# Broadcasts and sums in rounded parts, z gates in couples, a new order of filler units, and merge levels on half the columns, in a chain of transformer blocks

## The reference

```python
def first_block(...):
    x = x + 0.5 * swiglu(rms_norm(x, ffn1_norm), ...)
    x = x + hybrid_mixer(x, ...)
    x = x + 0.5 * swiglu(rms_norm(x, ffn2_norm), ...)
    return rms_norm(x, final_norm)

def second_block(...):
    for i in range(2):
        h = h + (gdn_mixer, sb_mixer)[i](rms_norm_2(h, ln_mix[i]), ...)
        h = h + swiglu_2(rms_norm_2(h, ln_ffn[i]), ...)
        h = h + (p[i] @ ple_w_proj[i]) * jax.nn.sigmoid(rms_norm_2(h, ln_ple[i]) @ ple_w_gate[i])
```

```python
    decay_mat = jnp.exp(jnp.where(causal, G[..., :, None] - G[..., None, :], -jnp.inf))
    a_low = jnp.where(strict, beta[..., None] * kk * decay_mat, 0.0)
    rhs = jnp.concatenate([v * beta[..., None], k * (beta * jnp.exp(G))[..., None]], axis=-1)
    sol = lax.linalg.triangular_solve(a_low + eye, rhs, lower=True, unit_diagonal=True)
```

## Time and profile before

| | us |
|---|---|
| median of 3 runs | 2642.24 (2640.12 to 2644.57) |
| profiled execution, its own time | 2639.76 |
| its span, first to last instruction | 2638.0 |
| PE busy | 2593.3 |
| DVE, ACT, POOL busy | 1041.8, 1089.7, 1060.8 |
| mean granted clock | 0.995 |

### The profile page before, as it was taken

How to read it: one execution, slowest core, us unless ns; L and a number is a source line. 1 busy time by engine, 2 the same in 40 slices (tenths; PEclk the granted TensorE clock), 3 DMA queues, 4 the chain that set the end, 5 groups by cost and what they waited for, 6 DMA issues and landing times.

```text
span 2638.0 us, 32543 instructions
## 1 busy us (share of the span) xinstructions
PE 2593.3 (98%) x12090; PEld 2100.3 (80%) x12090; DVE 1041.8 (39%) x1477; ACT 1089.7 (41%) x1567; POOL 1060.8 (40%) x466
## 2 busy tenths in 40 slices
PE   9999999999999999999999999999999999999999
PEld 7888887776888888777878878888877777888887
DVE  4212223966522122787456542122372344211224
ACT  5222233678432223565445542223355464222233
POOL 4444443222444444335334344444443222444444
PEclk9999999999999999999999999999999999999999
DMA  4232332111232222222000122322322112222233
GB/s 158 95 101 93 102 125 77 62 56 57 88 103 98 94 96 95 80 80 80 17 25 25 33 96 95 104 89 95 103 89 79 56 48 80 96 96 96 95 103 113
DMA packets 61719, 222.68 MB, mean 84 GB/s; under 512 B 6704, under 2 KB 6832, under 8 KB 61488
## 3 DMA queue, kind: packets, MB, share of 16 engines
q1 hardware_dynamic: 60928, 218.07, 25.0%
q10 hardware_dynamic: 688, 3.15, 0.3%
HBM read 219.10 MB, written 2.10 MB: 84 GB/s over the span
## 4 chain that ended last, share of the span: by engine, by line
PE 91%; DVE 6%; issue 2%; ACT 1%; DMA 0%; SPq 0%; DVEq 0%; ACTq 0%
PE ps L358 13%; PE ps L360 13%; PE ps L359 13%; PE ps L385 6%; PE ps L384 6%; PE ps L383 6%; PE ps L646 2%; PE ps L647 2%; PE ps L648 2%; PE ps L1471 1%; PE ps L1502 1%; PE ps L2187 1%; PE ps L1412 1%; PE ps L1414 1%; PE ps L1413 1%
## 5 line engine op out<-in xcount | busy, mean ns | idle before, releaser
L2470 POOL TENSOR_TENSOR w_lo<-raw,w_hi 128x1024 fp32r<-128x1024 f32 x405 | 981.9, 2426 | 1471.5 <-ACT w_hi L403 1471.5
L403 ACT ACTIVATE w_hi<-raw 128x1024 fp32r<-128x1024 f32 x405 | 424.9, 1050 | 468.2 <-PE ps L385 294.2
L358 PE MATMUL ps<-x_hi,w_hi 128*128 128x512 f32 x1536 | 600.7, 391 | 5.1 <-DVE x_lo L436 5.1
L359 PE MATMUL ps<-x_lo,w_hi 128*128 128x512 f32 x1536 | 597.7, 389 | 0.0
L360 PE MATMUL ps<-x_hi,w_lo 128*128 128x512 f32 x1536 | 597.6, 389 | 0.0
L358 PEld LDWEIGHTS ps<-x_hi,w_hi 128*128 128x128 f32 x1536 | 288.3, 188 | 69.9 <-DVE x_lo L436 6.7
L359 PEld LDWEIGHTS ps<-x_lo,w_hi 128*128 128x128 f32 x1536 | 288.3, 188 | 60.8 <-issue 1.4
L360 PEld LDWEIGHTS ps<-x_hi,w_lo 128*128 128x128 f32 x1536 | 288.3, 188 | 60.0
L383 PE MATMUL ps<-mid_hi,w_hi 128*128 128x512 f32 x736 | 286.3, 389 | 0.0
L384 PE MATMUL ps<-mid_lo,w_hi 128*128 128x512 f32 x736 | 286.3, 389 | 0.0
L385 PE MATMUL ps<-mid_hi,w_lo 128*128 128x512 f32 x736 | 286.3, 389 | 0.0
(11 more groups left out here) (371 smaller groups left out, 3814.1 us busy)
## 6 DMA issues: line engine op xcount, KB each, us to landing
raw<-in_units_dram SPq DMA_DIRECT2D x406, 512.0 KB, 3.5
h<-in_x_t_dram SPq DMA_DIRECT2D x4, 512.0 KB, 6.5
toep<-in_rel_table_dram ACTq DMA_DIRECT2D x1, 2048.0 KB, 9.1
out_dram<-h SPq DMA_DIRECT2D x4, 512.0 KB, 5.6
p_f<-in_p_t_dram ACTq DMA_DIRECT2D x2, 512.0 KB, 3.6
const<-in_constants_dram SPq DMA_DIRECT2D x1, 832.0 KB, 7.5
vec<-in_vectors_dram SPq DMA_DIRECT2D x1, 137.5 KB, 2.2
```

The lines of the kernel that those rows point to most:

```text
L358: nc.tensor.matmul(out, hi, x_hi[:, k, :], start=(k == 0), stop=False)
L359: nc.tensor.matmul(out, hi, x_lo[:, k, :], start=False, stop=False)
L403: nc.scalar.activation(w_hi[:, n % W_SLOTS, :], raw[:, n % RAW_SLOTS, :], ACT.Copy).then_inc(s_whi, 1)
L2470: nc.gpsimd.tensor_tensor(w_lo[:, n % W_SLOTS, :], raw[:, n % RAW_SLOTS, :], w_hi[:, n % W_SLOTS, :].bitcast(F32), ALU.subtract).then_inc( ...
```

## The change

1. *Broadcasts of mixers 1 and 2.* The rows are split into hi and lo parts which lie in one tile (`cs_parts`: hi in partitions 0 to 15, lo from 64; `g_parts`: hi from 0, lo from 64), and one fp32r product with K = 80 (K = 104) spreads their sum; its weights `sel` have two ones in a column. For that DVE does three instructions at x == 6 of mixer 1, ACT one and DVE two in mixer 2.
2. *z gates.* All of PE's gate pieces stand one m earlier; `z_silu` runs for two m at once between two decays; at m = 6 and 7 the pieces of an output unit take the place of gate pieces.
3. *Filler order.* In pair 1, gate 4 comes ahead of the output unit.
4. *Convolution tile 23* and its silu stand behind level 0 of pair 0.
5. *Merge levels.* Only half the columns of each block pattern hold anything new. Each 128x128x128 product becomes two with 64 weight columns and 64 moving columns (every second group of b columns), the two written to the two halves of the partitions. ACT's copy to `em`, DVE's subtraction and POOL's mask work on 256 columns instead of 512, and ACT writes zeros over the columns of `em` that the last level left (two copies a level). The turning to `tm` stays at 512 columns.
6. *Square sums of mixer 3.* hi and lo parts and two fp32r products; DVE squares, ACT copies to hi, DVE subtracts for lo.

The core of the diff:

```diff
...
-FILLS = ((("gate", 0), ("gate", 1), ("gate", 2)), (("gate", 3), ("out", 0, 0), ("gate", 4)),
+FILLS = ((("gate", 0), ("gate", 1), ("gate", 2)), (("gate", 3), ("gate", 4), ("out", 0, 0)),
...
+        sel = place("sel", 144 * KB + 1280 + len(MASKS) * P * 4, [P, 40], F32R)
...
+                    pe.wait_ge(s_sel, 1)
+                    pe.wait_ge(s_csp, 3)
                     pe.wait_ge(s_pt, 24)
                 elif x == 1:
                     pe.wait_ge(s_conv, 11)
                 else:
                     pe.wait_ge(s_m, x - 1)
-                nc.tensor.matmul(ps[:, SPREAD[x % 2], :], ident[0:SSD_HEADS, x:x + 1].to_broadcast([SSD_HEADS, P]), cs_row[:, :],
+                nc.tensor.matmul(ps[:, SPREAD[x % 2], :], sel[0:64 + SSD_HEADS, x:x + 1].to_broadcast([64 + SSD_HEADS, P]), cs_parts[:, :],
...
-            take(gates, 8)
+            take(gates, 16)
...
                 if m < 7:
                     x_turn(m + 1)
                     broadcast(2 * m + 2)
+                if m < 6:
                     take(gates, 4)
+                else:
+                    out_unit(n_t, 0, 0, (0, 1) if m == 6 else (2, 3))
+                if m < 7:
                     broadcast(2 * m + 3)
-                else:
-                    out_unit(n_t, 0, 0, (0, 1))
                 y_pair(m)
-                if m < 7:
+                if m < 6:
                     take(gates, 4)
             assert next(gates, None) is None
-            out_unit(n_t, 0, 0, (2, 3))
...
             z_silu(0)
+            z_silu(1)
             for m in range(8):
                 if m < 7:
                     decays(2 * m + 2)
+                if m in (2, 4, 6):
+                    z_silu(m)
+                    z_silu(m + 1)
+                if m < 7:
                     decays(2 * m + 3)
                 act.wait_ge(s_yg, m + 1)
                 if m >= 2:
                     act.wait_ge(s_ysum, m - 1)
                 nc.scalar.activation(sq[:, m % 2, :], zs[:, m, :], ACT.Square).then_inc(s_ysq, 1)
                 round_at(13 + m)
-                if m < 7:
-                    z_silu(m + 1)
...
+                        nc.vector.tensor_copy(cs_parts[0:SSD_HEADS, :], cs_row[:, :]).then_inc(s_csp, 1)
+                        dve.wait_ge(s_csp, 2)
+                        nc.vector.tensor_tensor(cs_parts[64:64 + SSD_HEADS, :], cs_row[:, :], cs_parts[0:SSD_HEADS, :].bitcast(F32), ALU.subtract).then_inc(s_csp, 1)
...
+        def halves(t, b, half):
+
+            return t.rearrange("p (g h b) -> p g h b", h=2, b=b)[:, :, half, :]
...
+        def level_out(j, part, b, c=None, side=None):
+
+            at, n_ = part * 2 * P + (c * 64 if c is not None else 0), 64 if c is not None else 2 * P
+            rows = slice(0, P) if side is None else slice(64 * side, 64 * side + 64)
+            return ps[rows, LEVEL[j], at:at + n_].rearrange("p (g b) -> p g b", b=b)
...
+                nc.tensor.matmul(ps[:, SETUP[j], :], sel[0:104, x:x + 1].to_broadcast([104, P]), g_parts[:, :], start=True, stop=True).then_inc(s_gbc, 1)
...
+                nc.tensor.matmul(ps[:, SETUP[j], :], sel[0:104, 32 + x:33 + x].to_broadcast([104, P]), g_parts[:, :], start=True, stop=True).then_inc(s_gbb, 1)
...
-                            last = nc.tensor.matmul(ps[:, LEVEL[j], c * P:(c + 1) * P], gw["ao"][j][:, c, :], gw["tm"][j][:, c, :], start=True, stop=True)
+                            for side in range(2):
+                                last = nc.tensor.matmul(level_out(j, 0, b, c, side), gw["ao"][j][:, c, 64 * side:64 * side + 64],
+                                                        halves(gw["tm"][j][:, c, :], b, 0), start=True, stop=True)
...
-                            last = nc.tensor.matmul(ps[:, LEVEL[j], c * P:(c + 1) * P], gw["em"][j][:, c, :], gw["tt"][j][:, c, :], start=True, stop=True)
+                            for side in range(2):
+                                last = nc.tensor.matmul(level_out(j, 1, b, c, side), gw["em"][j][:, c, 64 * side:64 * side + 64],
+                                                        halves(gw["tt"][j][:, c, :], b, 1), start=True, stop=True)
...
+                if u == 9:
+                    act.wait_ge(s_ga2, 2)
+                    nc.scalar.activation(g_parts[0:40, :], g_row[:, :], ACT.Copy).then_inc(s_gpt, 1)
...
+                    b = 2 << n
+                    for j in range(2):
+                        if n:
+                            act.wait_ge(s_gdp, level(p, n - 1, j))
+                            stale = wide(gw["em"][j]).rearrange("p (g h q b) -> p g h q b", h=2, q=2, b=b // 2)[:, :, 1, 0, :]
+                            nc.scalar.activation(stale, zero_col.rearrange("p (g b) -> p g b", b=1).to_broadcast([P, 2 * P // b, b // 2]), ACT.Copy)
+                        elif p:
+                            act.wait_ge(s_gdp, level(p - 1, 5, j))
+                            stale = gw["em"][j][:, :, 0:64].rearrange("p a (g h b) -> p a g h b", h=2, b=b)[:, :, :, 1, :]
+                            nc.scalar.activation(stale, zero_col.rearrange("p (a g b) -> p a g b", a=1, b=1).to_broadcast([P, NB, 16, 2]), ACT.Copy)
+                        else:
+                            act.wait_ge(s_gez, j + 1)
                     if n == 5:
                         for j in range(2):
                             act.wait_ge(s_gtp, 2 * p + j + 1)
-                            nc.scalar.activation(wide(gw["tm"][j]), ps[:, LEVEL[j], :], ACT.Copy).then_inc(s_gtm, 1)
+                            nc.scalar.activation(gw["tm"][j][:, :, 0:64], blocks(LEVEL[j])[:, :, 0:64], ACT.Copy).then_inc(s_gtm, 1)
                     for j in range(2):
                         act.wait_ge(s_gup, level(p, n, j))
-                        nc.scalar.activation(wide(gw["em"][j]), ps[:, LEVEL[j], :], ACT.Copy).then_inc(s_gu, 1)
+                        nc.scalar.activation(halves(wide(gw["em"][j]), b, 0), level_out(j, 0, b), ACT.Copy).then_inc(s_gu, 1)
...
+                            if x == 0:
+                                act.wait_ge(s_convact, 36)
...
                     if n == 0:
                         round_at(3 * p)
+                        if p == 0:
+                            conv_silu(23)
...
+                if u == 10:
+                    dve.wait_ge(s_gpt, 1)
+                    for at in (0, 32):
+                        nc.vector.tensor_tensor(g_parts[64 + at:72 + at, :], g_row[at:at + 8, :], g_parts[at:at + 8, :].bitcast(F32), ALU.subtract).then_inc(s_gpt, 1)
...
-                        nc.vector.tensor_tensor(gw["tt"][j][:, :, :], gw["tt"][j][:, :, :], blocks(LEVEL[j]), ALU.subtract).then_inc(s_gd, 1)
+                        upper_half = halves(wide(gw["tt"][j]), b, 1)
+                        nc.vector.tensor_tensor(upper_half, upper_half, level_out(j, 1, b), ALU.subtract).then_inc(s_gd, 1)
                         if n < 4:
                             dve.wait_ge(s_gd, level(p, n, j))
                             nc.vector.transpose(wide(gw["tm"][j]), wide(gw["tt"][j])).then_inc(s_gtm, 1)
+                    if p == 0 and n == 0:
+                        conv_tile(23, 24)
...
-                        nc.gpsimd.tensor_tensor(gw["ao"][j][:, :, :], gw["at"][j][:, :, :], merge, ALU.mult).then_inc(s_gao, 1)
+                        ao, at = (gw[name][j][:, :, :].rearrange("p a (g h b) -> p a g h b", h=2, b=b)[:, :, :, 1, :] for name in ("ao", "at"))
+                        nc.gpsimd.tensor_tensor(ao, at, merge, ALU.mult).then_inc(s_gao, 1)
...
-                nc.tensor.matmul(ps[:, 4 + c % 4, :], ones, n_sq3[:, c % 4, :], start=True, stop=True).then_inc(s_nsum, 1)
+                nc.tensor.matmul(ps[:, 4 + c % 4, :], ones_r[:, :], n_hi3[:, c % 4, :], start=True, stop=False)
+                nc.tensor.matmul(ps[:, 4 + c % 4, :], ones_r[:, :], n_lo3[:, c % 3, :], start=False, stop=True).then_inc(s_nsum, 1)
...
-                nc.scalar.activation(n_sq3[:, c % 4, :], src, ACT.Square).then_inc(s_nsq, 1)
+                nc.scalar.activation(n_hi3[:, c % 4, :], n_sq3[:, c % 3, :], ACT.Copy).then_inc(s_nhi, 1)
...
+            def square_lo(c):
+                dve.wait_ge(s_nhi, c + 1)
+                nc.vector.tensor_tensor(n_lo3[:, c % 3, :], n_sq3[:, c % 3, :], n_hi3[:, c % 4, :].bitcast(F32), ALU.subtract).then_inc(s_nsq, 1)
+
             for u in range(16):
                 dest = k3[:, u, :] if u < 8 else q3[:, u - 8, :]
                 dve.wait_ge(s_used, n0 + u + 1)
                 nc.vector.tensor_tensor(dest, ps[:, u % 4, :], rstd[:, :], ALU.mult).then_inc(s_free, 1)
+                if u >= 3:
+                    dve.wait_ge(s_nsum, SUMS + u - 2)
+                dve.wait_ge(s_free, b0 + u + 5)
+                nc.vector.tensor_tensor(n_sq3[:, u % 3, :], dest, dest, ALU.mult).then_inc(s_n32, 1)
+                if u:
+                    square_lo(u - 1)
...
+            nc.vector.tensor_tensor(sel[:, :], ident[:, 0:40], ident[:, 64:104], ALU.add).then_inc(s_sel, 1)
...
```

62 lines of the change are left out of this document (46 added, 16 removed).

## The result

The changed kernel takes 2591.53 us (median of 4 runs, 2590.54 to 2594.1) against 2641.18 us of the kernel before on the same chip: a ratio of 0.9815, 95% interval 0.9803 to 0.9828, 49.65 us or 1.9% less. The prediction said 2585 (2568 to 2606), so 56 to 57 us less. The profiled execution took 2591.75 us, its span is 2590.0 us.

What follows compares the result with a forecast made beforehand. TensorE, busy 98%, was taken to bound the kernel, through product time and waits with half clock. Savings 9.0 + 2.7 + 38.0 + 6.4 = 56.1 from 2639.8 gave 2583.7; it said 2585, range 2568 to 2606 (the sum's band 2577 to 2592).

Steps and rivals of the forecast that it cites:

- Price of a group: Merge levels: one head's products for one product of a level take 0.5 us (0.42 to 1.0) instead of 0.85.
- Rival 1: Merge levels: halves don't overlap, or load and issue bind; group stays 0.85 us, kernel 2603 (2599 to 2610); chance 0.18.
- rival 4: Merge levels: fixed time per small product, group from 1.25 us, kernel slower than before, 2676 at 1.6 a group; chance 0.04.
- The levels' sum, 38 us: Merge levels of all four pairs: 42.5 us less, 4.5 taken back for new waits, 38 saved (20 to 48).
- with gate 4 ahead of the out unit both go, 6.0: Pair 1: PE's 3.8 us wait for mid_lo and the 2.2 us half clock after it both vanish.
- pair 0's 5.9 - 4.3: Pair 0: moving tile 23 removes 5.9 us at level 0; late level 1 adds 3.3 wait and 1 half clock.
- There the other engines catch up: Merge levels: ACT's busy time in pairs 1 and 2 becomes 29.0 us, stretches 31.4, 3 to 4 above PE's work.
- Mixer 1, 9.0 us: Mixer 1, fp32r broadcasts and z gates in couples: 9 us saved, 5 to 15.4.
- ACT bounds: 9.18 us a period: Mixer 1's loop: ACT needs 9.18 us a period, PE 8.83, so ACT bounds; 7 periods save 11.0 us.
- Mixer 2's columns, 2.7 us: Mixer 2's column phase: four broadcasts in fp32r save 2.7 us, 1.5 to 3.8.
- Mixer 3, 6.4 us: Mixer 3's 16 square sums: 0.46 us each instead of 0.86, 6.4 us saved.
- the third rival: Change of product shape costs 8.6 us, or a fuller ACT and DVE as much: kernel 2594 (2592 to 2599); chance 0.16.

Runs made afterwards that it cites:

- experiment 1: Changed kernel with the 8 products of a merge-level group reordered, four for the lower partition half, then four for the upper: 2600.11 us, ratio 0.9853.
- experiment 2: Changed kernel with the merge levels as before the change, all else kept: 2619.8 us, ratio 0.993.
- experiment 4: Changed kernel with one stall put back at a time: gate 4 behind the output unit, 2593.78 us; convolution tile 23 ahead of the levels, 2596.03 us.
- experiment 3: Changed kernel without ACT's zeroing copies of em, so the delta rule is not computed: 2590.43 us.
- experiment 6: Changed kernel, mixer 1 broadcasts waiting only for ACT's decays: 2593.4 us; also with both broadcasts and both exponents early: 2599.07 us.
- Experiment 7: Changed kernel with ACT squaring and copying hi in mixer 3, DVE making only the lo part: 2590.12 us, ratio 0.9806.
- the second measurement: Changed kernel measured once more with no edit, against the kernel before on one chip: 2593.94 us, ratio 0.9823.

## Why the prediction was right, step by step

- **Price of a group.** Predicted 0.5 us (0.42 to 1.0), measured 0.54. 96 x 0.315 = 30 us, against 33.6. That `y_pair` was the right relative is shown by experiment 1: the overlap is that of neighbours on different halves. Rival 1 and rival 4 fell with it; their price would have been 0.85 and 1.25. The Trainium skill's statement on column tiles ("TensorE: Matmul & The Clock Gate", "Part 3: Packing small matmuls — row/col tiling"), by which the group was estimated at 0.45 us, is nearer than no overlap; the runs' 0.54 decides.
- **The levels' sum, 38 us.** Measured 38.0, but that is luck: the terms balance. The groups gave 28.7 us (experiment 2) where 33.6 was said. The 12 broadcasts took 12.0 us before and take 4.6 now (distances of starts without the waits), so they gave 7.4 for 8.7. The removed stalls and all new waits together gave the last 1.9, where 5.9 + 6.0 - 4.3 and, taken back, 7.4 for the other engines and 4.5 for new waits make -4.3. The step that failed is "with gate 4 ahead of the out unit both go, 6.0" and, smaller, pair 0's 5.9 - 4.3: put back, they cost 2.3 us in pairs 1 and 2 and 0.3 us in pair 0 (experiment 4), both within or near what these stretches vary by themselves. The new wait at level 1 was placed and sized well, 2.8 us for 3.3. A stall of PE here is mostly DVE's lateness, and it moves. The removed waits gave less than said and the new ones cost less than said.
- **"There the other engines catch up", ACT full.** The stretches of pairs 1 and 2 came out at 32.4 and 31.5 us for 31.4; the cause was another. ACT is busy for 25.0 us in each, not for 29.0; a zeroing copy takes 0.30 us, not 0.37. Without the zeroing nothing is gained (experiment 3), and PE's longest waits there are for `tm`, from DVE. That the loss stands where the removed stalls went is read from the lists of waits, not tested.
- **Mixer 1, 9.0 us.** Measured 7.7, and 3.8 to 7.7 over the traces in which this code is unchanged (stretches of 90.2 to 94.1). "ACT bounds: 9.18 us a period" failed: ACT is busy for 74.6 of 90.3 us, and a period takes 9.8 us (569.19 to 627.76 for six, the starts of the products ahead of each first broadcast). Three of the six take 9.3 us, which is PE's own work (8.83 was said); the others take 9.9 to 10.4, with the waits for multiplications of DVE that run beside POOL's `w_lo` (experiment 6). The prediction had nothing for that meeting. The tail was mis-sized in the other direction, 2.0 us of wait instead of 4. A broadcast was said to save 0.96 us; behind the f32 transposes of x it saves 1.0, ahead of the f32 y products 0.72, because the change to f32 now falls on its far side.
- **Mixer 2's columns, 2.7 us.** 0.9 in the pair of traces, and the stretch takes from 117.8 to 120.3 us in those of the other kernels, so its size isn't settled. The wait of 1.9 us at the first sum (L1401, now L1436) is still there, 3.2 us in the changed kernel and 1.9 to 3.3 in the others.
- **Mixer 3, 6.4 us.** Measured 3.7. The price of a sum was right (0.45 for 0.46). The step that failed is "DVE gets two operations of 0.69 under each unit": they take up to 2.9 beside POOL. The sentence on what a lost cover would cost, about 1 us a sum, is what happened at three of the 16 sums (0.82 us late and 0.11 slower each). Experiment 7 shows that DVE's load is the cause by taking one of its operations away; that POOL is what makes them long is read from the traces, no run moved POOL's work.
- **The sum.** 2583.7 us was said for an execution like the profiled one, and 2591.75 came: 1.3 us of mixer 1, 1.8 of the columns, 2.7 of mixer 3, and 2.2 of the three stretches that vary without an edit (2.0 - 1.5 + 1.7) make these 8.0. The measured gain of 49.65 us for 56 to 57 lies between the sum's band and the third rival's; the second measurement, 2593.94 us, is in the latter. Of that rival's two causes, the groups did come out 3.4 to 4.9 us dearer than said, whether by the change of shape wasn't measured; a fuller ACT and DVE came as single operations of DVE held up beside POOL.
